# The fourth sum product of the last pair ahead of the down tile, and its value block ahead of the gate's taps

## What is computed

```
up = xn @ w_up                              # 1024 -> 2 x 2816 columns
upc, new_buf = causal_dwconv(up, buf, cw, cb)   # width 3, per column
val, gate = split(upc)
x = x + (gelu(gate) * val) @ w_down         # 2816 -> 1024
y = rms_norm(x) * final_g                   # the last norm
```

## Time and profile before

| what | value |
|---|---|
| median of three runs | 1055.7 us |
| the profiled execution's own time | 1055.19 us |
| its span | 1053.4 us |
| PE busy | 1018.5 us, 97% of the span |
| DVE, ACT, POOL busy | 706.2, 520.5, 463.3 us |
| the mean granted clock of TensorE over the span | 0.988 |

### The profile page before, as it was taken

How to read it: one execution, slowest core, us unless ns; L and a number is a source line. 1 busy time by engine, 2 the same in 40 slices (tenths; PEclk the granted TensorE clock), 3 DMA queues, 4 the chain that set the end, 5 groups by cost and what they waited for, 6 DMA issues and landing times.

```text
span 1053.4 us, 20026 instructions
## 1 busy us (share of the span) xinstructions
PE 1018.5 (97%) x7688; PEld 992.8 (94%) x7688; DVE 706.2 (67%) x1236; ACT 520.5 (49%) x936; POOL 463.3 (44%) x320
## 2 busy tenths in 40 slices
PE   8999999999999999999999987999999999999995
PEld 7899999999999999999999977899999999999995
DVE  6787558947656467474735587887777777777653
ACT  7567786314434433432523454655455545454553
POOL 4333334342322222222133354777576656665630
PEclk9999999999999999999999998999999999999998
DMA  8533332468486786874543304322323232323137
GB/s 201 185 87 92 103 93 69 108 176 220 105 246 172 156 261 151 220 187 142 175 163 91 110 1 114 89 80 86 96 81 100 79 103 74 108 71 110 35 95 211
DMA packets 263268, 132.95 MB, mean 126 GB/s; under 512 B 82720, under 2 KB 257045, under 8 KB 262920
## 3 DMA queue, kind: packets, MB, share of 16 engines
q1 hardware_dynamic: 262966, 131.63, 45.7%
q10 hardware_dynamic: 210, 0.07, 0.0%
HBM read 104.17 MB, written 25.29 MB: 123 GB/s over the span
## 4 chain that ended last, share of the span: by engine, by line
PE 80%; issue 8%; DVE 5%; DMA 3%; POOL 2%; ACT 2%; SPq 0%; DVEq 0%; POOLq 0%; ACTq 0%
PE ring L2728 39%; PE bank L3119 12%; PE ring L3133 11%; PE ring L3119 8%; PE bank L2970 2%; POOL wlo L1221 2%; PE bank L2774 1%; PE bank L2953 1%; PE bank L3050 1%; PE bank L2881 1%; DMA y<-out_rows 1%; PE bank L3038 1%; DMA d_stage<-in_w_down 1%; PE bank L3133 1%; DMA f_stage<-in_w_up 1%
## 5 line engine op out<-in xcount | busy, mean ns | idle before, releaser
L1221 POOL TENSOR_TENSOR wlo<-stage,whi 128x1024 fp32r<-128x1024 f32 x78 | 199.1, 2553 | 402.0 <-ACT whi L1277 402.0
L2728 PE MATMUL ring<-x_split,whi 128*128 128x322 f32 (+2 forms) x1952 | 347.6, 300 | 0.1
L2728 PEld LDWEIGHTS ring<-x_split,whi 128*128 128x128 f32 x1952 | 294.5, 189 | 8.9 <-issue 8.1
L2728 PE MATMUL ring<-x_split,wlo 128*128 128x256 f32 (+1 forms) x976 | 210.5, 297 | 0.0
L1264 POOL TENSOR_TENSOR f_lo<-f_stage,f_hi 128x512 fp32r<-128x512 f32 x112 | 146.0, 1319 | 122.4 <-ACT f_hi L1658 122.4
L2728 PEld LDWEIGHTS ring<-x_split,wlo 128*128 128x128 f32 x976 | 164.6, 189 | 0.0
L1277 ACT ACTIVATE whi<-stage 128x1024 fp32r<-128x1024 f32 x79 | 83.3, 1054 | 81.3 <-PE ring L2728 70.4
L3119 PE MATMUL bank<-fx_T,f_hi 128*128 128x290 f32 x264 | 80.4, 304 | 10.7 <-ACT sum_one L1729 5.8
L3119 PE MATMUL bank<-fx_T,f_lo 128*128 128x290 f32 x264 | 79.1, 299 | 0.0
L3119 PE MATMUL bank<-fx_T_lo,f_hi 128*128 128x290 f32 x264 | 78.9, 299 | 0.0
L1658 ACT ACTIVATE f_hi<-f_stage 128x512 fp32r<-128x512 f32 x112 | 68.8, 624 | 10.4 <-DMA f_stage<-in_w_up 3.8
(11 more groups left out here) (429 smaller groups left out, 2333.1 us busy)
## 6 DMA issues: line engine op xcount, KB each, us to landing
stage<-in_w_in SPq DMA_DIRECT2D x56, 512.0 KB, 4.2
f_stage<-in_w_up SPq DMA_DIRECT2D x44, 512.0 KB, 5.4
d_stage<-in_w_down SPq DMA_DIRECT2D x40, 256.0 KB, 2.8
stage<-in_w_branch_a SPq DMA_DIRECT2D x8, 512.0 KB, 3.7
c_sample<-in_state_mlstm_C SPq DMA_DIRECT2D x16, 256.0 KB, 6.4
out_s_mlstm_C<-c_sample SPq DMA_DIRECT2D x16, 256.0 KB, 2.4
stage<-in_w_branch_b SPq DMA_DIRECT2D x8, 512.0 KB, 3.9
stage<-in_w_out SPq DMA_DIRECT2D x8, 512.0 KB, 3.6
```

The source lines that it names most:

```text
L1221: pool.tensor_tensor(spaced(wlo[:, slot]), packed(stage[:, slot, 0:n]), spaced(whi[:, slot]).bitcast(F32), ALU.subtract).then_inc(w_lo, 1)
L2728: last = pe.matmul(of(z, t0 or -2, t1), w[:, kk * WS:kk * WS + P], x_, start=kk == 0 and m == 0, stop=kk == kn - 1 and m == 2)
```

## The change

T4 of the last pair moves ahead of D(4,0): in the table of pieces, in ACT's list and on PE. On DVE, `two_one` of the last pair moves ahead of the gate's other taps. On ACT, the value tile's first tap moves ahead of the gelu, and `product_hi` moves ahead of two roundings.

```diff
@@ weight_order
     g0, g1 = GROUPS - 2, GROUPS - 1
+    yield "T4", NPAIR - 1
     yield "D", g0, 0
-    yield "T4", NPAIR - 1
     yield "D", g0, 1
@@ ScalarE, behind the loop over pairs
             first_tap(i, 1)
-            ahead("D", g0, 0)
-            gelu(i)
             ahead("T4", i)
             first_tap(i, 0)
+            gelu(i)
+            ahead("D", g0, 0)
+            product_hi(i)
             ahead("D", g0, 1)
             ahead("D", g0, 2)
-            product_hi(i)
@@ VectorE, behind the loop over pairs
             i = NPAIR
+            two_one(i - 1)
             other_taps(i - 1, 1)
-            two_one(i - 1)
             other_taps(i - 1, 0)
@@ TensorE, behind the loop over pairs
+            pe.wait_ge(sum_added, ADDED["C22", i])
+            up_product("T4", i, False)
             pe.wait_ge(tile_evicted, down_out_count(FINAL))
             down_product(g0, 0)
-            pe.wait_ge(sum_added, ADDED["C22", i])
-            up_product("T4", i, False)
```

## The result

The changed kernel takes **1057.36 us**, the median of 20 runs (1056.33 to 1060.29), against 1055.48 (1053.82 to 1057.45) for the kernel before in the same comparison. The ratio is 1.0018, 95% interval 1.0011 to 1.0024: 1.9 us slower, inside the 0.2% named above. The forecast was 1057.0. The profiled execution took 1057.11 us, with a span of 1055.3.

A forecast was written before the change was run, and what follows sets the result against it. PE, at work nearly the whole span, was taken to bound the kernel. The profiled 1055.19 plus 1.0 (balance) and 0.3 (clock) gave 1056.5; the median lies 0.5 above, so 1057.0 us, range 1055.4 to 1058.9.

The forecast's parts named there:

- T4's release: PE before T4: C22's addition on DVE comes no earlier, so PE stands still 3.8 us until 997.83.
- ACT's delay: ACT, pair 21's step: D(4,1)'s rounding starts 0.25 us later (0.2 to 0.75); high part, C22 and T4 follow.
- POOL and SP: POOL's splits and the load of D(4,2): nothing added to T4's delay, by a margin of 0.4 us only.
- The later wait: PE before D(5,0)'s second half: the 1.90 us wait for DVE's last low part goes in full.
- The balance of 1.0 us: PE at D(5,0)'s second half, at full clock: 1009.88 against 1008.88, 1.0 us later.
- PE waits for nothing again until the last sums: PE behind 1009 us: no further waits until the last sums, so a shift reaches the end in full.
- the read-back moves along: The transfer reading stored outputs back (1036.89, 7.59 us) shifts with PE, so PE's shift reaches the end in full.
- The clock: PE behind its gaps: one slow stretch behind T4 replaces that behind D(5,0), 1.7 against 1.7 us; small term 0.3.
- The term of 0.3 us: Clock on PE: the kernel before sometimes spared its slow stretch, one in five, the changed one hardly ever; 0.3 us.
- The longer low stretch: Rival, PE behind T4: the longer gap holds the clock down longer, up to 1058.4 or 1058.9 us; chance 0.18.
- C22 early: Rival, DVE: C22's addition right behind T3, T4 at about 994.7, 0.9 and 1.7 us saved, 1053.1; chance 0.02.
- The later wait stays: Rival, PE at D(5,0): loads ahead on ACT hold the low part; two gaps, second slow stretch, 1058.4; chance 0.04.

The follow-up runs named there:

- the kernel with T4 back: The changed kernel with T4 put back behind D(4,0) on PE and in ACT's roundings, the other edits kept: 1056.16 us, ratio 1.0006.
- with the turn moved: The changed kernel with T4 put back behind D(4,0), and PE's `f_last` transposition one pair of down pieces later: 1053.65 us, ratio 0.9984.
- the kernel before with the later turn: The kernel before with only PE's transposition of `f_last` one pair of down pieces later: 1054.87 us, ratio 0.9996.

## Why the prediction was right, and where it failed

**T4's release: right.** The gap was worked out as 3.8 us and is 3.79. It was read from who releases T4: `product_lo`, ACT's high part, D(5,0)'s rounding and its load, none of which the change brings forward. The kernel with T4 alone moved has the same gap (3.75), and the one with the addition ahead of the low part a shorter one (2.46).

**ACT's delay: right in its sum, by luck in its parts.** 0.25 was worked out and 0.27 measured. But the prediction put all of it on the rounding of D(4,1), and this starts only 0.08 us later, counted from T3's end (991.78 for 991.19). The load behind it took 2.18 us instead of 2.03, which is most of the rest:

```profile
991.78 0.62 ACT L1658 ACTIVATE f_hi<-d_stage 128x512 fp32r<-128x512 f32 x1
```

```profile
993.86 2.18 DMA d_stage<-in_w_down
```

**POOL and SP: right for T4**; D(4,2)'s rounding ends at 995.36, and D(5,0)'s load releases ACT at 996.06, a margin of 0.7 us where 0.4 was worked out.

**The later wait: right.** It went in full, with 3.1 us to spare, and the edits on DVE and ACT cost nothing. What the prediction left open is which of them matter: with T4 alone moved 1.24 us of the wait stay, so the place of `product_hi` is a condition of the sum. The same edit has a price that the sum doesn't name, since D(4,4)'s rounding now stands behind it: nothing in the change, where that rounding still waits 0.27 us for PE, and about 0.8 us by the estimate above in the kernel with T4 back.

**The balance of 1.0 us: right.** PE comes to the turn 1.06 us later.

**"PE waits for nothing again until the last sums": this step failed.** It was read from PE's waits of the kernel before, which show no row there. A missing row says that a wait is met, not by how much: the margin was 0.2 us. In the kernel before PE took 16.6 us from D(4,1)'s end (1002.67) to the turn, the gap of 1.90 us and the low clock behind it among them; with both gone it takes 12.7, and the 13.1 us of loads, rounding, square, gain and transposition that begin at D(4,1) are longer. In the change this costs PE a wait of 0.46 us. That the time of the change is longer by it is not shown: without the wait it is 1.8 us over the kernel before all the same. In the kernel with T4 back the wait of 2.68 us did decide the result: with the turn moved the ratio falls from 1.0006 to 0.9984, and the intervals lie apart. The step's second half, "the read-back moves along", holds for PE's shift of 1.58 us to the later side (the end moves by 1.39) and fails to the earlier side (3.70 and 1.85).

**The clock: right in kind, and its small term bears checking.** One stretch of 3.4 us moved from D(5,0) to T4; it costs PE some 1.5, where 1.7 was worked out. The term of 0.3 us rests on gaps of about 2 us sometimes sparing the clock. They do, and this is how it looks in the kernel before with the later turn:

```profile
1009.57 0.53 PE L3133 MATMUL ring<-gh,f_hi 128*128 128x280 f32 x2 [2.38 <-DVE gl L2632]
```

```profile
1009.60:1013.00 3.40, 3.40 (x26) 3.40 (x27) 1.05 (x7) 1.31 (x3) 1.47 (x2) 1.00 0.18 49
```

The gap is longer than 1.90 and the clock behind it full. In the stretches read around the change, gaps of 1.84, 1.90, 1.99, 2.07, 2.46 and 2.84 us were followed by a low clock, and 2.38 and 2.68 were not: two in eight. That is near the one in five assumed, but not for the reason given, that 1.90 lies near the gap of 1.3 that spared the clock: the four shortest of the eight all lowered it. All four empty gaps of 3.65 us and more were followed by it. So the rule weighed above, by which each wait throttles the clock anew, holds for most of these gaps and not for all.

The mean granted clock of every execution is on record too: 0.9875 over the 20 of the change, 0.9891 over 96 of the kernel before. The difference of 0.0016 is what one stretch of 3.4 us at half pace takes from 1055 us (1.7 us). So the kernel before seems to lose about one stretch less per execution, which is more than one in five, unless stretches elsewhere differ too, which a mean can't tell. In its time this does not show: of the 96, the 34 executions with a clock of 0.988 or less have a median of 1055.05 us, the 38 with 0.990 or more one of 1055.03. So neither the one in five nor the 0.3 us is shown.

**The sum.** 1.0 and 0.3 were forecast and 1.9 measured, between medians. The profiled executions bear out 1.06 for the first. With the wait of the failed step PE's last sums are 1.58 us late, of which 1.39 reach the end of the span; the other 0.5 us of the 1.9 stay open. That the forecast came within 0.4 us is in part luck: it lacked a wait, and the size of its clock term is not shown.

**The rivals.** The longer low stretch didn't come: 3.4 us, as behind every other gap around the change that lowered the clock. C22 early didn't come, for the reason given against it; made early by hand, it gave T4 1.3 us and the kernel nothing. The later wait stays in the kernel with T4 alone: two gaps, 1058.6 where the rival had 1058.4. The number agrees by luck, since the rival's price was a second low stretch and the second gap, of 1.24 us, had none behind it.

## What to carry to other kernels

A product moved ahead in an in-order list gained nothing here, since what releases it came no earlier: follow its releaser back before moving it, and leave ready work in front of it to fill the wait. Before counting a gain on the engine that bounds, look behind it for the next waits that are just met, which have no row in the profile: compare the end of each needed result with the start of its user. And compare two traces from an event ahead of the first edit, or half a microsecond of something else enters the sum.

## What the runs showed of the hardware that was not expected

DVE's two value taps (L1868, in `val_taps`), whose operands lie in SBUF, took longer where POOL's splits ran beside them. At 1004.06 in the kernel before they take 1.71 us with no split beside them; in the kernel after, the two at 991.04 take 3.42 us. POOL after:

```profile
989.49 1.30 POOL L1264 TENSOR_TENSOR f_lo<-weight_sum_T,f_hi 128x512 fp32r<-128x512 f32 x1 [2.73 <-ACT f_hi L1658]
990.75 1.29 POOL L1264 TENSOR_TENSOR f_lo<-d_stage,f_hi 128x512 fp32r<-128x512 f32 x1
992.48 1.35 POOL L1264 TENSOR_TENSOR f_lo<-d_stage,f_hi 128x512 fp32r<-128x512 f32 x1 [0.43 <-ACT f_hi L1658]
```

POOL is at work for 2.3 of the 3.42 us. The same taps on the gate's tile, which lies in a PSUM bank, took 1.71 us in the kernel before at 1000.54, with a split beside them from 1001.14 on. The Trainium skill (page "SBUF — State Buffer", section "Who interferes with whom") says that a DVE instruction with two SBUF inputs contends with a GpSimd instruction that reads SBUF; the trace agrees, with 1.7 us more for two instructions. No run here varied it by itself. It took most of the slack on DVE ahead of the low part (0.61 us of idle time left, where the earlier trace rows have 2.39), so by these rows over 0.6 us more of it would have set T4's start.
